# The residual of the first down chunk added by transfers, and a chunk's loads and operand parts in the order of use

## The reference, cut to what matters

```
def conv_ffn(h, w_up, w_conv, b_conv, w_down, conv_state):
    up = h @ w_up                                   # D_MODEL 1024 -> 2 * D_FF, D_FF = 2816
    a, val = jnp.split(up, 2, axis=-1)
    a_ext = jnp.concatenate([hist, a], axis=1)
    c = b_conv + sum(w_conv[i] * a_ext[:, i:i + S] for i in range(CONV_W))
    out = (jax.nn.gelu(c) * val) @ w_down           # 2816 -> 1024
    return out, a_ext[:, -(CONV_W - 1):]
...
x = x + merged @ w_o[l]                             # called x1 below
f, conv_new = conv_ffn(rms_norm(x, ln_ffn_g[l]), ...)
x = x + f
y = rms_norm(x, ln_final_g)
```

## Time and profile before

| | us |
|---|---|
| median of 3 runs (lowest, highest) | 1651.01 (1650.73, 1655.04) |
| the profiled execution's own time | 1649.72 |
| its span in the profile | 1647.9 |
| PE busy | 1614.5 (98%) |
| DVE busy, ACT busy | 1152.0 (70%), 706.7 (43%) |

### The profile page before, as it was taken

One profiled execution on the slowest core, in us unless ns is written; L12 is line 12 of the kernel. 1 busy time (PEld: TensorE's weight loads), 2 busy tenths in 40 slices (PEclk: granted clock), 3 DMA queues, 4 the chain that ended last, 5 costly groups with the idle time before them and its releaser, 6 DMA issues. The chain is left out here.

```text
span 1647.9 us, 32421 instructions
## 1 busy us (share of the span) xinstructions
PE 1614.5 (98%) x12886; PEld 1574.7 (96%) x12886; DVE 1152.0 (70%) x2078; ACT 706.7 (43%) x1292; POOL 71.7 (4%) x141
## 2 busy tenths in 40 slices
PE   6999999999999999999999999999999999999998
PEld 6999999999999999999999999999999999999997
DVE  6566565656658868696525888888888776767566
ACT  7344444444444336364434534444333334343312
POOL 2000000000000000001112100000000000000001
PEclk8999999999999999999999999999999999999999
DMA  7444434343437864757743233333333427363122
GB/s 248 151 150 118 133 107 137 102 138 100 119 111 204 242 215 161 246 161 169 166 135 99 59 115 97 107 106 106 106 106 107 131 72 266 120 241 105 69 78 110
DMA packets 272472, 227.03 MB, mean 138 GB/s; under 512 B 43335, under 2 KB 223363, under 8 KB 272323
## 3 DMA queue, kind: packets, MB, share of 16 engines
q1 hardware_dynamic: 138750, 154.36, 28.2%
q10 hardware_dynamic: 131269, 66.15, 14.3%
q0 software_dynamic: 2304, 4.46, 1.7%
HBM read 150.56 MB, written 74.36 MB: 136 GB/s over the span
## 5 line engine op out<-in xcount | busy, mean ns | idle before, releaser
L2296 PE MATMUL ps<-op_hi,w_hi 128*128 128x272 f32 x3672 | 775.6, 292 | 15.5 <-issue 5.6
L2296 PE MATMUL ps<-op_hi,w_lo 128*128 128x272 f32 x3672 | 760.6, 289 | 0.0
L2296 PE MATMUL ps<-op_lo,w_hi 128*128 128x272 f32 x3672 | 758.6, 288 | 0.0
L2296 PEld LDWEIGHTS ps<-op_hi,w_hi 128*128 128x128 f32 x3672 | 576.1, 189 | 32.7 <-issue 30.2
L2296 PEld LDWEIGHTS ps<-op_lo,w_hi 128*128 128x128 f32 x3672 | 578.0, 189 | 0.0
L2296 PEld LDWEIGHTS ps<-op_hi,w_lo 128*128 128x128 f32 x3672 | 575.0, 189 | 0.0
L1608 DVE TENSOR_TENSOR w_lo<-raw,w_hi 128x512 fp32r<-128x512 f32 x256 | 173.7, 698 | 157.2 <-ACT w_hi L1201 157.2
L1201 ACT ACTIVATE w_hi<-raw 128x512 fp32r<-128x512 f32 x256 | 153.7, 625 | 134.1 <-PE ps L2296 90.1
L1280 ACT ACTIVATE u<-ps 128x544 f32<-128x544 f32 x106 | 66.2, 624 | 237.6 <-PE ps L2296 237.4
L1201 ACT ACTIVATE w_hi<-w_f 128x512 fp32r<-128x512 f32 x159 | 95.3, 625 | 39.6 <-DVE w_f L1628 30.4
L1608 DVE TENSOR_TENSOR w_lo<-w_f,w_hi 128x512 fp32r<-128x512 f32 x159 | 104.8, 683 | 3.9 <-ACT w_hi L1201 3.4
(11 more groups left out here) (191 smaller groups left out, 1514.1 us busy)
## 6 DMA issues: line engine op xcount, KB each, us to landing
in_spill<-quad SPq DMA_DIRECT2D x88, 272.0 KB, 2.3
raw<-in_w_up_dram ACTq DMA_DIRECT2D x44, 512.0 KB, 4.7
raw<-in_w_in_dram ACTq DMA_DIRECT2D x42, 512.0 KB, 5.4
g_spill<-value_out SPq DMA_DIRECT2D x22, 544.0 KB, 2.7
t_spill<-t_buf SPq DMA_DIRECT2D x8, 1088.0 KB, 4.3
lo_f<-g_spill SPq DMA_DIRECT2D x8, 1088.0 KB, 7.9
lo_f<-t_spill SPq DMA_DIRECT2D x8, 1088.0 KB, 9.3
raw<-in_w_down_dram ACTq DMA_DIRECT2D x16, 512.0 KB, 5.2
```

What stands on the lines that cost most here:

```text
L2296: last = pe.matmul(out[:, h, 0:HB], (w_hi, w_lo)[a][place][:, j, :], (op_hi, op_lo)[b][at][:, j, HB * h:HB * h + HB], start=fresh and j == ...
```

## The change

- The four `load_xy` are gone. The quadrants of chunk 0 are written into xyp directly: in pair 56 by ACT (`quadrant_out`, a copy of the region), in pairs 57 to 59 by DVE's `combine` from the copy and the region, without `add_copy`. Then POOL adds x1 to each finished tile by an accumulating transfer of 1088 KB (`add_x1`), placed in pairs 57 to 60, when all four quadrants of the pair before are written (s_comb). Chunk 1 adds onto the tiles as before, and waits for these transfers.
- The loads of operands 2, 3 and 5 move from the pair before a chunk into its first pair, behind 7 and 6, and the load of 2 waits for the weights of the chunk's second pair.
- The high and low parts are made later and in the order of use: operand 0's low part now stands behind `combine` of Q22, and 2, 3, 5, 4 one slot or more later.
- In pair 57 `value_scale`, `gated_value` and `store_g` stand later.

```diff
@@ sp
                     if n == 2:
                         sp.wait_ge(s_gt_out, 16 * KP * (c + 1))
+                        sp.wait_ge(s_raw, 32 * (FIRST_PAIR[g] + 2))
-            def load_xy(i):
-                if i == 0:
-                    stored(UP)
-                    sp.wait_ge(s_op, OP_BASE[5])
-                    sp.wait_ge(s_gt_out, 16 * KP * NCHUNK)
-                if i == 2:
-                    sp.wait_ge(s_g_out[1], 16 * (FT // 2))
-                    sp.wait_ge(s_tail, FT)
-                sp.dma_start(xyp[i][:], x1_spill[2 * i:2 * i + 2].rearrange("k p t -> p k t")).then_inc(s_x1_in[i], 16)
...
-                    if p == FIRST_PAIR[g] - 1 and j == 0 and 0 < n:
-                        load_chunk(g, (0, 1, 2, 3, 7, 5)[n - 1])
...
+                    if p == FIRST_PAIR[g] - 1 and j == 0 and n in (1, 2, 5):
+                        load_chunk(g, {1: 0, 2: 1, 5: 7}[n])
+                    if p == FIRST_PAIR[g] and (n, j) in ((0, 1), (2, 0), (2, 2), (3, 0), (5, 0)):
+                        load_chunk(g, {(0, 1): 6, (2, 0): 2, (2, 2): 3, (3, 0): 5, (5, 0): 4}[n, j])
@@ gpsimd
+            def add_x1(i):
+                for q in range(4):
+                    pool.wait_ge(s_q_out[q], 16 * store_count(q, UP))
+                pool.wait_ge(s_comb, 4 * (DOWN + i + 1))
+                pool.dma_start(xyp[i][:], x1_spill[2 * i:2 * i + 2].rearrange("k p t -> p k t"), accum_op=ALU.add)\
+                    .then_inc(s_x1_in[i], 16)
...
+                if DOWN < p <= DOWN + 4 and (n, j) == (1, 0):
+                    add_x1(p - 1 - DOWN)
@@ scalar, operand_hi
-                        todo = {(4, 0): (0,), (5, 2): (1,)}.get((n, j), ())
+                        todo = {(4, 2): (0,), (5, 2): (1,)}.get((n, j), ())
...
@@ scalar, quadrant_out
-                            if plain(p) and stage(p) != "down" and k in (3, 4, 7):
+                            if plain(p) and p <= DOWN and k in (3, 4, 7):
                                 quadrant_out(p, {3: Q11, 4: Q21, 7: Q12}[k])
@@ vector
+                if kind == "down":
+                    if p == DOWN + 1:
+                        dve.wait_ge(s_gt_out, 16 * KP * NCHUNK)
+                    if p == DOWN + 2:
+                        dve.wait_ge(s_g_out[1], 16 * (FT // 2))
+                    if p == DOWN + 3:
+                        dve.wait_ge(s_tail, FT)
...
-                elif stage(p) == "down":
+                elif p >= DOWN + 4:
                     out = destination(p, q)
                     dve.wait_ge(s_xadd, copies_added(p, q))
...
-                if p < DOWN + 4:
-                    dve.wait_ge(s_x1_in[p - DOWN], 16)
+                dve.wait_ge(s_x1_in[p - DOWN - 4], 16)
@@ vector, operand_lo
-                        lows = {(4, 3): (0,), (6, 1): (1,)}.get((n, j), ())
+                        lows = {(5, 1): (0,), (6, 2): (1,)}.get((n, j), ())
...
-                    if (n, j) == (2, 1):
+                    if (n, j) == ((2, 1) if p < DOWN else (3, 3)):
                         value_scale(f)
-                    if (n, j) == (3, 2):
+                    if (n, j) == ((3, 2) if p < DOWN else (5, 2)):
                         gated_value(f)
```

More of the change, by code:

```diff
@@ L1009, in background @@
                 f = ffn_tile(p)
-                if f is not None and (n, j) == (5 if f == 0 else 4, 2):
+                if f is not None and (n, j) == (5 if f == 0 else 4 if p < DOWN else 6, 2):
                     store_g(f)
@@ L1364, in free_place @@
                                 act.wait_ge(s_t3, t3_count(2))
+                if kind == "down":
+                    act.wait_ge(s_op, OP_BASE[5])
+                    act.wait_ge(s_q_out[Q12], 16 * store_count(Q12, UP))
                 if kind == "up":
@@ L1546, in _ @@
                         if (k, j) == (0, 0):
-                            if p and plain(p - 1) and stage(p - 1) not in ("out", "down"):
+                            if p and plain(p - 1) and stage(p - 1) != "out" and p <= DOWN + 1:
                                 quadrant_out(p - 1, Q22)
@@ L1757, in copies_added @@
             def copies_added(p, q):
-                return 4 * sum(not plain(m) for m in range(DOWN, p)) + ADDED.index(q) + 1
+                return 4 * sum(not plain(m) for m in range(DOWN + 4, p)) + ADDED.index(q) + 1
             def add_copy(p, q):
-                if p < DOWN + 4:
-                    dve.wait_ge(s_x1_in[p - DOWN], 16)
+                dve.wait_ge(s_x1_in[p - DOWN - 4], 16)
                 dve.wait_ge(s_copied, COPIES_BEFORE[p] + MADE[q][3])
@@ L2117, in last_quadrant @@
                     residual_out(p, Q22)
-                elif stage(p) == "down":
+                elif p == DOWN + 4:
                     down_out(p, Q22)
@@ L2134, in base @@
                         residual_out(p, {3: Q11, 4: Q21, 7: Q12}[k])
-                    if kind == "down" and j == 0 and k in (3, 4, 7):
+                    if p == DOWN + 4 and j == 0 and k in (3, 4, 7):
                         down_out(p, {3: Q11, 4: Q21, 7: Q12}[k])
@@ L2147, in base @@
                             add_residual(p, Q21)
-                    if kind == "down" and (n, j) in ((1, 2), (3, 2)):
+                    if p > DOWN + 4 and (n, j) in ((1, 2), (3, 2)):
                         add_copy(p, Q11 if n == 1 else Q12)
-                    if kind == "down" and (n, j) == (5, 0):
+                    if p > DOWN + 4 and (n, j) == (5, 0):
                         add_copy(p, Q22)
```

12 lines of the change are left out of this document (2 added, 10 removed).

## The result

Side by side on one chip the changed kernel took 1663.37 us (median of 4 runs, 1661.82 to 1664.77), the kernel before 1652.17 (4 runs). The ratio is 1.0067, 95% interval 1.0054 to 1.008: slower by 11.2 us. It lies outside the predicted range, 2.9 us above its upper end; 1.2 of that is the kernel before, whose median was 1651.01 in the prediction. Among the rivals it is nearest to the third, with some more on top.

A forecast was written before the change was run, and what follows sets the result against it. PE, busy 98% of the span, was taken to bound the kernel. Terms -8.5 + 4.6 + (2.9 + 1.7) + 2.3 = +3.0 us on the median 1651.01 gave 1654.0 us, with an 8-in-10 range of 1644 to 1660.5.

The forecast's parts named there:

- the third: Rival: x1 goes wholly ahead of the weights, d = 6.8, both later waits slow the clock; +8.3 us, 1659.3; chance 0.23.
- What goes: Three PE gaps, in pairs 55 and 59 and ahead of 57, go with the clock behind the second: -8.5 us.
- DVE, SP, `gated_value`, `store_g`, x1 of pair 60 at nothing: Work leaving DVE and SP's queue, the later gated_value and store_g, and x1 asked for in pair 60: priced at nothing.
- Pair 57: New PE wait of 2.9 at product k = 2 for ACT's copy behind convolve; with clock it costs 4.6 us.
- The 1.7 of clock: Cost of the low clock expected behind pair 57's wait, and likewise behind pair 59's: 1.7 us each.
- d: Delay of weights by a whole x1 transfer beside them in pairs 59 and 60: between 3.8 and 6.8, taken as 5.0 us.
- the prediction's own price: Accumulating merges of 272 KB: 1.09 MB take 6.7 us of all engines.
- The upper bound: Top value of d, 6.8 us: all of an x1 transfer goes ahead of the weights.
- Pair 59: PE wait of d - 2.1 = 2.9 us for Q22, weights issued 0.65 earlier; 1.7 of clock on top.
- Ahead of pair 61: PE wait of 2.3 us for Q12, as loads 2 and 3 wait for pair 61's weights; no clock added.
- The sum: All forecast terms together: -8.5 + 4.6 + (2.9 + 1.7) + 2.3 = +3.0 us.

The follow-up runs named there:

- 12: The kernel before with one line changed, DVE making operand 0's low part behind Q22 in pairs 55 and 59: ratio 1.0007.
- experiment 1: The kernel before with only the new order of chunk loads and operand parts and load 2's wait for weights, x1 as before: ratio 0.998.
- 4: The changed kernel with the later x1 transfers of experiment 3, and ACT's first copy m1c ahead of convolve in pair 57: ratio 0.9966 to the kernel before.
- experiment 3: The changed kernel, its second to fourth x1 transfers also waiting for the weights of pairs 59, 62 and 63: ratio 0.9983 to the kernel before.
- 5: The changed kernel with only the third x1 transfer moved, behind the fourth and pair 62's weights: ratio 1.0023 to the kernel before.
- 7: The changed kernel with x1's four transfers plain instead of accumulating, the first chunk's residual left out: ratio 0.998 to the kernel before.
- 11: The changed kernel, its second to fourth x1 transfers also waiting for the end of their pair's second product: ratio 1.0012 to the kernel before.
- 6: The changed kernel with only the fourth x1 transfer moved, behind pair 63's weights: ratio 1.0022 to the kernel before.
- 8: The changed kernel without load 2's wait for weights, which pair 57's chunk loads lost too: ratio 1.0136 to the kernel before.
- 10: As 4, with gelu of tile 21 behind ACT's second copy in pair 57, but without load 2's wait for weights: ratio 1.001 to the kernel before.
- experiment 2: The kernel before with only the accumulating x1 transfers and ACT's copies of chunk 0's quadrants, loads and parts in the old order: ratio 1.0072.

## Why the prediction was wrong, point by point

- **What goes.** Right in the changed kernel: 0.15 left in pair 55, Q12's gap gone. The reason was incomplete. Moving the low part wins nothing by itself (12); in experiment 1 the whole new order takes those gaps, and ACT's copies of Q12 weren't needed for that.
- **DVE, SP, `gated_value`, `store_g`, x1 of pair 60 at nothing.** PE has no wait for them in the trace from 1340 to 1570; no run tests them by themselves.
- **Pair 57.** Forecast a wait of 2.9 for m1c, measured 3.11, by the chain that was counted (4). The 1.7 of clock behind it came in the profiles of experiments 1, 3, 5, 7 and 11, not in that of 6 nor in the changed kernel's.
- **d, the step that failed.** The mechanism was right, that x1 beside the weights holds up the chain to Q22 and to Q12; its size was not. d was taken as 5.0, between 3.8 and 6.8, and the waits in pair 59 and ahead of pair 61 with it; it was 6.8 (18.07 - 11.27). The value was read off medians of two landings. Before, the weights issued at 764.1 had a median of 8.3, but ACT used them 10.1 behind their issue:

```profile
774.16 1.15 ACT L1201 ACTIVATE w_hi<-raw 128x512 fp32r<-128x512 f32 x2 [2.63 <-DMA raw<-in_w_pa_dram]
```

By the same median the changed kernel's weights took 8.1, which would make d 3.6. Nor did the merges hold the weights up "by most of their own time": by the prediction's own price two of them take 3.4, and the delay was 3.8 with plain loads beside. These rows gave no value for a whole x1.
- **The upper bound was right by its number, and in part by luck.** It took x1 for 6.8 of all engines, by the price of merges with packets of 2 KB, and put all of it ahead. Measured, x1 takes 5.6, comes 4.3 behind its issue and passes packet for packet with the weights. Its 17 packets per engine are far fewer than the weights' 130, so it is through before the last of them. What makes d 1.2 more than x1's own time no run takes apart. The rival's odds of 0.23 were too low, and its condition, d above 5.6, was met.
- **Pair 59.** 2.9 forecast, 5.54 measured: 1.8 from d, and most of the rest because the weights were issued 2.1 behind the pair's start as before (2.2), not 0.65 earlier: their last low part on DVE ran as late as ever. With the clock it is 7.3 against the 4.6.
- **Ahead of pair 61.** 2.3 forecast, 5.66 measured: 1.8 from d, some 0.7 because the weights landed 15.2 behind the pair's start where 12.7 + 1.8 = 14.5 was counted, and 0.9 because PE started 14.55 behind them, not 13.65. The clock fell in this gap too and cost 1.5, which I had put at nothing.
- **The sum.** The third rival's +8.3, less the 1.7 of clock in pair 57, with 0.4, 0.9 and 1.5 more in pairs 57, 59 and 61, 0.15 in pair 55 and the 2.1 upstream, gives 11.6; the difference of the spans is 11.5.
- **The Trainium skill's rule** on the queues (DMA: Bandwidth & Descriptors, Queues, rings and completion order) gave the third rival its d of 6.8. The runs side with it in the result. They don't show its turns of 9 to 17 descriptors: x1 and the weights alternated packet for packet, or nearly.

## What to carry to other kernels

Ask of every bulk transfer whose landing is waited for: which queues run beside it, and how many packets per engine each has. With equal turns the one with the most packets per engine, here the one with the smallest, lands last, behind the whole of the others; so place bulk transfers that nobody awaits behind both the small-packet transfer and the load that it releases (3 against 11), and keep a wait that holds loads back (8, 10) until a run has shown that it costs something. A gap of the bounding engine that has a queue of work behind its releaser is not gone when one item is moved out of its way; follow the order to the next place where that engine is asked (12, 4).

## What the runs showed that I had not expected

- Removing one wait on SP made a gap of 5.66 one of 13.41: the weights landed 26 us behind their issue, where both were there after 5.7 when alone (experiment 3).
- An accumulating x1 transfer takes 5.6 us of all engines, a plain one of as many packets 2.8, at the same place beside the weights.
- A gap's length doesn't settle what the clock does behind it. Gaps of 2.38 (experiment 2), 2.77 (7), 2.96 (3), 2.97 (before), 3.06 and 3.15 (11), 3.14 (5) and 3.35 (1) were followed by about 3.4 us at 1.2 GHz; gaps of 2.78 (6), 3.11 (changed kernel) and 3.25 (11) were not. None up to 2.00 was, all from 3.92 on were. And the clock was low from about 916 on in five of the 14 profiles (changed kernel, 5, 6, 8 and 12) with no gap near, which costs 1.7 and tells nothing of the kernel.
